# The first block's recurrent unit, cut into steps between the items of its attention, and a small product of the recurrence placed behind two transposes

## The chip, the cores and the metric

The kernel runs on one core of a Trainium2 chip. The metric is the device time of one execution in microseconds (us). A core has a matrix engine (PE in the views, TensorE), a vector engine (DVE), an activation engine (ACT), a general one (POOL), and a queue engine that only starts transfers (SP). Each works through its own list of instructions in order; semaphores make one wait for another. Matrix products go from the on-chip memory (here one big tile called arena) to eight banks of an accumulator memory (psum).

## The reference, cut to what matters

Two transformer-like blocks follow one another, all in 32-bit floats: 512 tokens, width 1024. The first block projects its input to six streams. Two of them go through a convolution and a gated linear recurrence (the recurrent unit), four through an attention with 8 heads; both results are normed, joined and projected.

```python
xa = causal_depthwise_conv(xa, conv_w, conv_b)
r = sigmoid(einsum(xa, w_a) + b_a);  i = sigmoid(einsum(xa, w_x) + b_x)
a = exp(-8 * r * softplus(-lam));    u = sqrt(1 - a * a) * (i * xa)
h[t] = a[t] * h[t-1] + u[t]
ya = rms_norm(h * silu(ga))
yb = rms_norm(dilated_attention(q, k, v) * silu(gb))
x = x + gate * rms_norm(concat(ya, yb) @ w_out)
```

The second block mixes a pooling branch, a differential attention and a two-way delta-rule recurrence, and ends in a mixture of 32 experts. In that recurrence every token also gets a bonus, whose coefficient is a product summed over each head's 64 channels: `coef = sum(r * k_mod * r_k)` per head.

## The kernel before, in words

The program is written out by hand for each engine; the order of the code is the order of the work. The stages of the first block are the modulation rows (`pre_`), the projections (`proj1_`), the recurrent unit (`lru_`), the attention (`att_`) and the output (`out1_`).

The recurrent unit works on four blocks m of 128 channels by 512 tokens. For each, DVE does the convolution (one `ts`, three `stt` of 512 elements per partition, signal `xc`), PE two gate products, ACT two sigmoids, then an exponential and a tanh (`th`), DVE an addition and a reciprocal (`rec`), two products (`ms`), ACT a square root, DVE a product, the scan and a product (`ya`). One block ends before the next begins, since all use the tiles tm[0] to tm[4]. After the fourth come the squares (`rsq`), a product with ones (`rs`), a root (`rsr`), a reciprocal and four scalings (`yan`). A short piece on 128x4 tiles ahead of it computes softplus(lam) on DVE.

The attention goes over 32 items x = (i, h): query tile i of 128 tokens and head h, with n = 128 (i + 1) keys. An item is a score product (`s1`), on DVE an addition of the mask and a maximum (`m1`), on ACT the exponential (`p1`), on PE i + 1 transposes (`pt1`), on ACT a copy, on PE i + 1 products with the values (`pv1`). The loop is skewed: in pass x PE does the scores of item x, the transposes of x - 2 and the values of x - 3. After each eighth item comes the output of query tile i: on DVE a reciprocal and two products (`yg`), on ACT a square and a root (`yr`), on DVE the norm (`yb`), then four transposes on PE.

Into both stages PE weaves the ada steps: 12 chunks of modulation weights, each 2 MB loaded by SP, in three steps q. Steps 0 and 1 are four products each with 32 output rows and 512 columns, step 2 adds a bias and gathers rows (two products with one or two output rows). 16 of the 36 steps stand in the recurrent unit, four behind each block's gates, and 20 in the attention, one per pass.

Psum banks are handed out in turn from a ring (`ps.take`): a new user waits until the one that had the bank is done with it. The recurrent unit has a ring of seven banks (LBANK), the attention one of five (ABANK), the ada steps one bank.

In the second block's recurrence two directions d, six chunks n each, are interleaved in a fixed order of steps; between the steps PE computes products of another stage (128x512, the gates of the merge). For a chunk, step g2 is 16 products into two banks, step kn transposes two key tiles into two banks, which ACT copies out. Each direction has a ring of only two banks. The coefficient product `co` has four matmuls with 8 columns; DVE adds or copies the result. It is there for 8 chunks (`lat`: four in each direction).

Of the kernel before, what the change touches and what calls it, by code (L numbers as in the profile page):

```python
# [11 lines left out]
ALU = mybir.AluOpType  # L12
ACT = mybir.ActivationFunctionType
# [319 lines left out]
def build(nc, T_):  # L333
# [18 lines left out]
    with ctx:  # L352
# [492 lines left out]
        def lru_gpsimd():  # L845
            G.wait_ge(T["f1", 3, 1])
            G.dma(wbd, T_["w_rg"], d_wbd.up("wbd"))
            G.dma(nbb, T_["norm_att"].partition_broadcast(128), d_na.up("na"))
            for j in range(4, 16):
                ada_gpsimd(j)  # L850

        def lru_tensor():
            steps = iter(ADA)
            for m in range(4):
                for j in range(2):
                    T.wait_ge(V["xc", m], d_wbd["wbd"], *ps.take(LBANK, "gate", m, j))
                    T.mm(ps["gate", m, j], wbd[:, c4(4 * j + m)], XC[:, m, :], True, True).then_inc("gate", m, j)
                for _ in range(4):
                    ada_tensor(*next(steps), MBANK)
            T.wait_ge(*ps.take(LBANK, "rs"))  # L860
            for m in range(4):
                T.wait_ge(A["rsq", m])
                T.mm(ps["rs"], ones, tm[m % 2], m == 0, m == 3).then_inc("rs", m)
            return steps

        def lru_scalar():
            steps = iter(ADA)
            A.wait_ge(V["lw1"])
            A.act(lw[2], lw[1], ACT.Exp).then_inc("lw2")
            for m in range(4):  # L870
                for j, (bn, tmp) in enumerate((("b_a", tm[0]), ("b_x", tm[1]))):
                    A.wait_ge(T["gate", m, j])
                    A.act(tmp, ps["gate", m, j], ACT.Sigmoid, bias=P[bn][:, m:m + 1])
                    ps.free(A.last(), "gate", m, j)
                A.wait_ge(V["lw"])
                A.act(tm[2], tm[0], ACT.Exp, scale=lw[7][:, m:m + 1])
                A.act(tm[3], tm[0], ACT.Tanh, scale=lw[6][:, m:m + 1]).then_inc("th", m)
                A.wait_ge(V["ms", m])
                A.act(tm[3], tm[3], ACT.Sqrt).then_inc("ms", m)
                for _ in range(4):  # L880
                    ada_scalar(*next(steps))
            A.wait_ge(V["ya", 3])
            for m in range(4):
                if m > 1:
                    A.wait_ge(T["rs", m - 2])
                A.act(tm[m % 2], XC[:, m, :], ACT.Square).then_inc("rsq", m)
            A.wait_ge(T["rs", 3])
            A.act(tm[2], ps["rs"], ACT.Sqrt, bias=eps[:, 0:1], scale=1.0 / 512).then_inc("rsr")
            ps.free(A.last(), "rs")
            return steps  # L890

        def lru_vector():
            lam, cw = P["lam"], P["conv_w"]
# [15 lines left out]
            for m in range(4):  # L909
                xc = XC[:, m, :]  # L910
                V.wait_ge(A["xa", m])
                V.ts(xc, XA[:, m, 1:513], cw[:, m:m + 1], P["conv_b"][:, m:m + 1], ALU.mult, ALU.add)
                for k in range(1, 4):
                    V.stt(xc, XA[:, m, 1 + k:513 + k], cw[:, 4 * k + m:4 * k + m + 1], xc, ALU.mult, ALU.add)
                V.then_inc("xc", m)
# [8 lines left out]
                V.tt(xc, tm[4], GA[:, m, :], ALU.mult).then_inc("ya", m)  # L924
            V.wait_ge(A["rsr"])
            V.rec(tm[2], tm[2])
            for m in range(4):
                V.stt(XC[:, m, :], XC[:, m, :], P["norm_rec"][:, m:m + 1], tm[2], ALU.mult, ALU.mult)
            V.then_inc("yan")
# [4 lines left out]
        def att_tensor(steps):  # L934
# [1843 lines left out]
```

## Time and profile before

| | |
|---|---|
| median of 3 runs | 2268.76 us (2268.49 to 2268.77) |
| the profiled execution, its own time | 2265.61 us |
| its span, first to last instruction | 2263.5 us |
| PE busy over the span | 1902.4 us (84%) |
| DVE, ACT busy | 814.9 us (36%), 519.8 us (23%) |
| mean granted TensorE clock | 0.893 |

The span is the time between the first and last instruction of the profiled execution; its own time contains 2.1 us more. The clock is the share of TensorE's full speed that was granted: 1.00 is 2.4 GHz and 0.50 is 1.2 GHz, and a value between them is a mixture over the window. PE's busy time is modelled at its ends, so that a busy PE need not be one at full rate.

### The profile page before, as it was taken

To read this page: it belongs to the slowest core of one execution; us is meant where nothing else is said; L and a number is where in the kernel's file an instruction comes from. 1 tells how busy PE (TensorE), PEld (TensorE's weight loads), DVE (VectorE), ACT (ScalarE), POOL (GpSimd) and SP (SyncE) were. 2 spreads that over 40 slices of the span, in tenths; PEclk is the share of its full clock that TensorE was granted. 3 is DMA by queue.
4 is the path that set the end of the run, shared out by engine and by line. 5 is a ranking of instruction groups with operands and counts; after the bars stand their busy time and mean duration, and the time that the engine had idled before them with its cause. 6 is when DMAs were issued, how large, how long until landed. Compare 5 with 4: busy or idle time off the path is not lost.

```text
span 2263.5 us, 29709 instructions
## 1 busy us (share of the span) xinstructions
PE 1902.4 (84%) x12822; PEld 1001.8 (44%) x12822; DVE 814.9 (36%) x1359; ACT 519.8 (23%) x957; POOL 82.5 (4%) x117
## 2 busy tenths in 40 slices
PE   5998569998998789978889889999974977777773
PEld 2443114643444555546666666664443332333231
DVE  2031533354645726434444544435335100000002
ACT  3001444321114512153233233113000000000001
POOL 0000000000000000020000000000000000000002
PEclk8999677599998899988899889999985999999997
DMA  8222343035111031031211111216415999999996
GB/s 338 75 74 75 112 159 139 27 137 218 59 37 38 0 135 47 0 127 43 67 49 54 62 43 49 90 35 270 159 64 224 416 428 426 426 427 426 428 427 242
DMA packets 49618, 376.37 MB, mean 166 GB/s; under 512 B 6033, under 2 KB 6177, under 8 KB 30795
## 3 DMA queue, kind: packets, MB, share of 16 engines
q1 hardware_dynamic: 36571, 317.85, 35.1%
q0 software_dynamic: 10032, 46.08, 5.6%
q10 hardware_dynamic: 2880, 10.49, 1.1%
q8 instruction: 103, 1.69, 0.3%
q14 instruction: 32, 0.26, 0.0%
HBM read 347.08 MB, written 31.51 MB: 167 GB/s over the span
## 4 chain that ended last, share of the span: by engine, by line
PE 40%; DMA 11%; DVE 8%; issue 2%; ACT 2%; POOL 0%; SPq 0%; DVEq 0%; ACTq 0%; POOLq 0%
PE psum L202 39%; DMA arena<-in_w 10%; DVE arena L149 4%; ACT arena L199 2%; DVE arena L159 1%; PE psum L205 1%; DVE arena L179 1%; DVE arena L167 1%; DVE arena L154 1%; DMA arena<-in_tok 0%; DVE arena L183 0%; DVE arena L187 0%; DVE arena L163 0%; DMA arena<-yd,arena 0%; DVE arena L175 0%
## 5 line engine op out<-in xcount | busy, mean ns | idle before, releaser
L202 PE MATMUL psum<-arena 64*64 64x32 f32 (+9 forms) x12174 | 1813.3, 372 | 303.0 <-ACT arena L199 104.2
L202 PEld LDWEIGHTS psum<-arena 64*64 64x64 f32 (+4 forms) x12174 | 922.5, 157 | 1135.3 <-issue 905.4
L199 ACT ACTIVATE arena<-psum 128x512 f32<-128x512 f32 (+6 forms) x389 | 206.5, 531 | 1195.9 <-PE psum L202 1083.2
L149 DVE TENSOR_TENSOR arena<-arena,psum 128x512 f32<-128x512 f32 (+1 forms) x136 | 75.5, 555 | 647.0 <-ACT arena L199 403.3
L199 ACT ACTIVATE arena<-arena 128x512 f32<-128x512 f32 (+10 forms) x242 | 135.4, 559 | 344.0 <-DVE arena L149 137.5
L149 DVE TENSOR_TENSOR arena<-arena 128x512 f32<-128x512 f32 (+11 forms) x312 | 195.4, 626 | 35.8 <-DMA arena<-in_norm_post 8.9
L149 DVE TENSOR_TENSOR arena<-psum,arena 128x256 f32<-128x256 f32 (+2 forms) x114 | 58.1, 509 | 253.8 <-PE psum L202 249.9
L159 DVE SCALAR_TENSOR_TENSOR arena<-arena 128x512 f32<-128x512 f32 (+5 forms) x138 | 111.4, 807 | 67.1 <-ACT arena L199 62.5
L205 PE MATMUL psum<-arena 128*128 128x128 f32 x648 | 108.3, 309 | 25.8 <-DVE arena L159 18.4
L205 PEld LDWEIGHTS psum<-arena 128*128 128x128 f32 x648 | 81.3, 157 | 93.3 <-issue 53.1
L199 ACT ACTIVATE arena<-psum,arena 128x128 f32<-128x128 f32 (+3 forms) x157 | 82.6, 526 | 173.0 <-PE psum L202 132.8
L167 DVE RECIPROCAL arena<-arena 128x1 f32<-128x1 f32 (+5 forms) x71 | 79.1, 1114 | 87.8 <-ACT arena L199 84.9
L154 DVE TENSOR_SCALAR arena<-arena 128x768 f32<-128x768 f32 (+9 forms) x156 | 50.0, 320 | 116.6 <-ACT arena L199 111.6
L199 ACT ACT_TABLE_LOAD x67 | 86.0, 1283 | 19.5 <-DMA arena<-gd 12.3
L163 DVE COPY arena<-psum 128x512 f32<-128x512 f32 (+2 forms) x76 | 47.6, 626 | 56.6 <-PE psum L202 31.1
L159 DVE SCALAR_TENSOR_TENSOR arena<-psum,arena 128x512 f32<-128x512 f32 (+3 forms) x44 | 23.7, 538 | 63.8 <-PE psum L202 62.6
L175 DVE TENSOR_REDUCE arena<-psum 128x1 f32<-128x768 f32 x32 | 30.7, 958 | 41.0 <-PE psum L202 38.5
L183 DVE STREAM_TRANSPOSE arena<-arena 128x512 f32<-128x512 f32 x60 | 42.7, 712 | 2.1
L179 DVE COPY_PREDICATED arena<-arena,psum 128x512 f32<-128x512 uint32 (+1 forms) x48 | 30.5, 636 | 25.4 <-PE psum L202 21.1
L142 POOL DMA_INDIRECT arena<-fd,arena x16 | 15.2, 948 | 512.7 <-PE psum L205 366.4
L139 POOL DMA_DIRECT2D arena<-kd x28 | 20.8, 750 | 341.5 <-DVE arena L149 328.4
L175 DVE TENSOR_REDUCE arena<-arena 128x1 f32<-128x32 f32 (+8 forms) x61 | 25.3, 414 | 6.1 <-PE psum L202 3.8
(46 smaller groups left out, 111.4 us busy)
## 6 DMA issues: line engine op xcount, KB each, us to landing
arena<-in_w SPq DMA_DIRECT2D x133, 2048.0 KB, 29.0
arena<-in_w SPq DMA_DIRECT2D x48, 256.0 KB, 3.0
yd<-arena ACTq DMA_DIRECT2D x16, 512.0 KB, 10.4
arena<-kd POOLq DMA_DIRECT2D x28, 256.0 KB, 3.9
gd<-arena SPq DMA_DIRECT2D x24, 256.0 KB, 3.1
arena<-gd SPq DMA_DIRECT2D x24, 256.0 KB, 8.4
yd<-in_zeros SPq DMA_DIRECT2D x1, 4096.0 KB, 18.6
arena<-in_w POOLq DMA_DIRECT2D x2, 2048.0 KB, 9.4
```

The lines of the kernel that those rows point to most:

```text
L139: self.e.dma_start(out, in_).then_inc(*signal)
L149: return self.ends(self.e.tensor_tensor(out, a, b, op))
L154: return self.ends(self.e.tensor_scalar(out, a, s1, None, op0))
L159: return self.ends(self.e.scalar_tensor_tensor(out=out, in0=a, scalar=s, in1=b, op0=op0, op1=op1))
L163: return self.ends(self.e.tensor_copy(out, a))
L167: return self.ends(self.e.reciprocal(out, a))
L175: return self.ends(self.e.tensor_reduce(out, a, AX, op, negate=negate))
L179: return self.ends(self.e.copy_predicated(out, mask, a))
L183: return self.ends(self.e.transpose(out, a))
L199: return self.ends(self.e.activation(out, a, func, **kw))
L202: return self.ends(self.e.matmul(out, lhs, rhs, start=start, stop=stop))
L205: return self.ends(self.e.transpose(out, a, ident))
```

## The change

The recurrent unit is no longer a stage of its own. Its functions now take a pass number x and do one piece of the work in that pass of the attention's loop. Block m has its gate products on PE and its sigmoids on ACT in pass 7m + 2, exponential and tanh in 7m + 3, addition and reciprocal on DVE in 7m + 4, the two products in 7m + 5, the root in 7m + 6, scan and products in 7m + 7. The convolutions are in passes 0 to 7, the final norm in passes 29 to 34. The softplus piece stays ahead of the loop on DVE. All 36 ada steps are in the attention, one per pass, and two in pass 1. PE computes the scores of item x + 1 in pass x; the score tile and the statistics have three buffers instead of two. The gate weights have memory of their own, so POOL starts their load and that of the attention's norm vector at once instead of behind the first transposes. Gates and `rs` take banks from ABANK. The transfers of out1 now wait for `yan` too. In the recurrence `co` stands behind the transposes of step kn, on PE and on DVE. The diff, cut:

```diff
 def lru_gpsimd():
-    G.wait_ge(T["f1", 3, 1])
     G.dma(wbd, T_["w_rg"], d_wbd.up("wbd"))
     G.dma(nbb, T_["norm_att"].partition_broadcast(128), d_na.up("na"))
...
-wbd = r0[:, 0:1024]
+wbd, Sb3, Pb3, sqj = ar.get(1024), ar.get(512), ar.get(512), ar.get(512)
-Sb, Pb, PTb, YB = sl[0:2], [sl[2], sl[3], tm[3]], sl[4:6], sl[6:8]
+Sb, Pb, PTb, YB = [*sl[0:2], Sb3], [sl[2], sl[3], Pb3], sl[4:6], sl[6:8]
...
-def lru_tensor():
-    steps = iter(ADA)
-    for m in range(4):
+def lru_tensor(x):
+    m = (x - 2) // 7
+    if x % 7 == 2 and m < 4:
         for j in range(2):
-            T.wait_ge(V["xc", m], d_wbd["wbd"], *ps.take(LBANK, "gate", m, j))
+            T.wait_ge(V["xc", m], d_wbd["wbd"], *ps.take(ABANK, "gate", m, j))
             T.mm(ps["gate", m, j], wbd[:, c4(4 * j + m)], XC[:, m, :], True, True).then_inc("gate", m, j)
-        for _ in range(4):
-            ada_tensor(*next(steps), MBANK)
-    T.wait_ge(*ps.take(LBANK, "rs"))
-    for m in range(4):
...
+    if x in (30, 31):
+        if x == 30:
+            T.wait_ge(*ps.take(ABANK, "rs"))
+        for m in (2 * x - 60, 2 * x - 59):
             T.wait_ge(A["rsq", m])
             T.mm(ps["rs"], ones, tm[m % 2], m == 0, m == 3).then_inc("rs", m)
...
+def lru_vector(x):
+    if x < 8:
...
+    m = (x - 4) // 7
+    if x % 7 == 4 and 0 <= m < 4:
         V.wait_ge(A["th", m])
         V.ts(tm[4], tm[3], 1.0, None, ALU.add)
         V.rec(tm[4], tm[4])
+    if x % 7 == 5 and 0 <= m < 4:
         V.stt(tm[3], tm[3], 2.0, tm[4], ALU.mult, ALU.mult).then_inc("ms", m)
-        V.tt(tm[1], tm[1], xc, ALU.mult)
+        V.tt(tm[1], tm[1], XC[:, m, :], ALU.mult)
+    m = x // 7 - 1
+    if x % 7 == 0 and 0 <= m < 4:
         V.wait_ge(A["ms", m])
         V.tt(tm[1], tm[1], tm[3], ALU.mult)
         V.scan(tm[4], tm[2], tm[1])
-        V.tt(xc, tm[4], GA[:, m, :], ALU.mult).then_inc("ya", m)
+        V.tt(XC[:, m, :], tm[4], GA[:, m, :], ALU.mult).then_inc("ya", m)
+    if x == 33:
         V.wait_ge(A["rsr"])
         V.rec(tm[2], tm[2])
+    if x == 34:
...
+scores(0)
 for x in range(len(IT1) + 3):
-    if x < len(IT1):
-        i, h = IT1[x]
+    if x + 1 < len(IT1):
+        scores(x + 1)
+    lru_tensor(x)
...
-    if (jq := next(steps, None)) is not None:
-        ada_tensor(*jq, MBANK)
+    for _ in range(1 + (x == 1)):
+        ada_tensor(*next(steps), MBANK)
...
-    n, o, s = 128 * (i + 1), LNC_OFF[i], Sb[x % 2]
+    n, o, s = 128 * (i + 1), LNC_OFF[i], Sb[x % 3]
     V.wait_ge(T["s1", x])
-    if x > 1:
-        V.wait_ge(A["p1", x - 2])
+    if x > 2:
+        V.wait_ge(A["p1", x - 3])
...
+lru_vector(x)
 if x % 8 == 4 and x > 8:
     gated((x - 12) // 8)
...
-    if step == "g2" and lat(d, n):
-        T.wait_ge(V["e2", d, n], *ps.take(ring, "co", d, n))
-        for m in range(4):
-            T.mm(ps["co", d, n][:, 0:8], B.e2[:, m, :], IRK[:, m, :], m == 0, m == 3)
-        T.then_inc("co", d, n)
 elif step == "kn":
     for j in range(2):
         T.wait_ge(*ps.take(ring, "kn", d, n, j))
         for m in range(4):
             T.tr(ps["kn", d, n, j][:, c4(m)], B.KB[:, j, m, :], ident)
         T.then_inc("kn", d, n, j)
+    if lat(d, n):
+        T.wait_ge(V["e2", d, n], *ps.take(ring, "co", d, n))
+        for m in range(4):
+            T.mm(ps["co", d, n][:, 0:8], B.e2[:, m, :], IRK[:, m, :], m == 0, m == 3)
+        T.then_inc("co", d, n)
...
-    elif lat(d, n):
+elif step == "kn":
+    if lat(d, n):
         V.wait_ge(T["co", d, n])
```

On DVE, at the beginning of the recurrent unit (the rows of 128x4 tiles end the softplus piece; 128x512 are tiles of the recurrent unit), there stood before:

```order
L159 SCALAR_TENSOR_TENSOR arena<-arena 128x4 x2
L154 TENSOR_SCALAR arena<-arena 128x4 x2
L155 TENSOR_SCALAR arena<-arena 128x512
L159 SCALAR_TENSOR_TENSOR arena<-arena 128x512 x3
L154 TENSOR_SCALAR arena<-arena 128x512
L167 RECIPROCAL arena<-arena 128x512
```

and now, where the rows that read psum are the scores of items 0 to 2, and the reductions their maxima:

```order
L159 SCALAR_TENSOR_TENSOR arena<-psum,arena 128x128
L175 TENSOR_REDUCE arena<-arena 128x1
L155 TENSOR_SCALAR arena<-arena 128x512
L159 SCALAR_TENSOR_TENSOR arena<-arena 128x512
L159 SCALAR_TENSOR_TENSOR arena<-psum,arena 128x128
L175 TENSOR_REDUCE arena<-arena 128x1
L159 SCALAR_TENSOR_TENSOR arena<-arena 128x512 x2
L159 SCALAR_TENSOR_TENSOR arena<-psum,arena 128x128
L175 TENSOR_REDUCE arena<-arena 128x1
```

The convolution is split in two pieces, and a score row and a maximum stand ahead of each.

On PE, in the recurrence, around the first coefficient product (64x128 are the products of step g2, 128x8 is `co`, 128x512 the woven products, L205 the transposes of the keys; the brackets name the semaphores waited for), there stood before:

```order
L202 MATMUL psum<-arena 64x128 [waits s_dve]
L202 MATMUL psum<-arena 64x128 x15
L202 MATMUL psum<-arena 128x8 [waits s_dve]
L202 MATMUL psum<-arena 128x8 x3
L202 MATMUL psum<-arena 128x512 [waits d_gw2,s_act]
L202 MATMUL psum<-arena 128x512
L202 MATMUL psum<-arena 64x32 x16
L202 MATMUL psum<-arena 64x64 x16
L202 MATMUL psum<-arena 128x512 x2
L205 MATMUL psum<-arena 128x128 [waits s_dve]
L205 MATMUL psum<-arena 128x128 x3
```

and now:

```order
L202 MATMUL psum<-arena 64x128 [waits s_dve]
L202 MATMUL psum<-arena 64x128 x15
L202 MATMUL psum<-arena 128x512 [waits d_gw2,s_act]
L202 MATMUL psum<-arena 128x512
L202 MATMUL psum<-arena 64x32 [waits s_dve]
L202 MATMUL psum<-arena 64x32 x15
L202 MATMUL psum<-arena 64x64 x16
L202 MATMUL psum<-arena 128x512 x2
L205 MATMUL psum<-arena 128x128 [waits s_dve]
L205 MATMUL psum<-arena 128x128 x3
L205 MATMUL psum<-arena 128x128 [waits s_dve]
L205 MATMUL psum<-arena 128x128 x3
L202 MATMUL psum<-arena 128x8 [waits s_act]
```

The product has moved behind the transposes, and what it waits for at its bank is ACT instead of DVE.

## Rows read from the trace of the kernel before

**Rows 1.** The page: span, busy tenths in 40 slices of 56.6 us.
```profile
span 2263.5 us, 29709 instructions
...
PE   5998569998998789978889889999974977777773
...
PEclk8999677599998899988899889999985999999997
DMA  8222343035111031031211111216415999999996
```

**Rows 2.** Windows of the two stages: busy us (instructions) by engine, clock, DMA share, GB/s.
```profile
217.50:318.30 100.80, 49.47 (x146) 10.24 (x144) 54.14 (x80) 41.74 (x51) 2.57 (x5) 0.71 0.39 143
318.30:356.00 37.70, 33.70 (x146) 11.63 (x146) 12.04 (x32) 18.70 (x50) 2.03 (x4) 0.86 0.55 195
356.00:370.00 14.00, 14.00 (x42) 4.58 (x41) 2.54 (x6) 4.30 (x13) 0.51 (x1) 0.51 0.23 97
370.00:387.00 17.00, 15.55 (x73) 6.46 (x72) 7.98 (x15) 9.67 (x20) 0.50 (x1) 0.99 0.33 124
387.00:447.30 60.30, 55.23 (x180) 38.48 (x180) 20.84 (x35) 23.76 (x49) 0.51 (x1) 0.50 0.00 1
```

**Rows 3.** Timeline of DVE, one block of channels: start us, busy us, idle before and releaser.
```profile
225.72 0.55 DVE L155 TENSOR_SCALAR arena<-arena 128x512 f32<-128x512 f32 x1
226.30 2.33 DVE L159 SCALAR_TENSOR_TENSOR arena<-arena 128x512 f32<-128x512 f32 x3
236.07 0.43 DVE L154 TENSOR_SCALAR arena<-arena 128x512 f32<-128x512 f32 x1 [7.45 <-ACT arena L199]
236.53 3.35 DVE L167 RECIPROCAL arena<-arena 128x512 f32<-128x512 f32 x1
...
254.82 0.43 DVE L154 TENSOR_SCALAR arena<-arena 128x512 f32<-128x512 f32 x1 [7.75 <-ACT arena L199]
```

**Rows 4.** Timeline of ACT in the same block.
```profile
233.26 1.28 ACT L199 ACT_TABLE_LOAD   x1
234.56 1.48 ACT L199 ACTIVATE arena<-arena 128x512 f32<-128x512 f32 x2
```

**Rows 5.** Timeline of PE in the attention, columns as in rows 3.
```profile
343.10 2.06 PE L202 MATMUL psum<-arena 128*32 128x512 f32 x12
...
363.17 4.13 PE L202 MATMUL psum<-arena 128*32 128x512 f32 x14
...
387.21 3.12 PE L202 MATMUL psum<-arena 128*128 128x64 f32 x8 [1.66 <-ACT arena L199]
...
429.36 3.81 PE L202 MATMUL psum<-arena 128*128 128x64 f32 x10
...
447.29 1.12 PE L205 MATMUL psum<-arena 128*128 128x128 f32 x4 [4.87 <-DVE arena L159]
```

**Rows 6.** Windows of the start, columns as in rows 2.
```profile
0.00:28.20 28.20, 8.23 (x44) 2.29 (x46) 0.81 (x6) 7.50 (x13) 1.48 (x6) 0.94 0.94 371
```

**Rows 7.** Timeline of PE at the start.
```profile
28.16 4.62 PE L202 MATMUL psum<-arena 128*32 128x512 f32 x24 [5.46 <-DMA arena<-in_w]
```

**Rows 8.** Timeline of POOL at the start.
```profile
36.63 0.53 POOL L139 DMA_DIRECT2D arena<-in_w_rg  x1 [34.05 <-PE psum L205]
```

**Rows 9.** Groups by form, 975 to 1525 us: busy, mean ns, idle before by releaser.
```profile
L202 PE MATMUL psum<-arena 128*128 128x8 f32 x64 | 12.3, 320 | 16.4 <-DVE arena L179 16.4
```

**Rows 10.** Timeline of PE around one coefficient product.
```profile
1260.44 7.77 PE L202 MATMUL psum<-arena 128*128 128x8 f32 x57 [3.06 <-DVE arena L179]
```

**Rows 11.** Timeline of DVE at the same place.
```profile
1259.65 1.59 DVE L179 COPY_PREDICATED arena<-arena,psum 128x512 f32<-128x512 uint32 x2
```

**Rows 12.** Timeline of ACT: two copies of transposed keys.
```profile
1050.00 1.29 ACT L199 ACTIVATE arena<-psum 128x512 f32<-128x512 f32 x2
```

**Rows 13.** Timeline of SP: the experts' weight loads.
```profile
1608.18 185.28 SPq L139 DMA_DIRECT2D arena<-in_w  x20
```

**Rows 14.** Window of the recurrence, columns as in rows 2.
```profile
975.00:1525.00 550.00, 500.14 (x8031) 345.76 (x8031) 247.93 (x421) 174.26 (x348) 28.11 (x41) 0.91 0.19 62
```

More of the change, by code:

```diff
@@ L874, in lru_scalar @@
                     ps.free(A.last(), "gate", m, j)
+            if x % 7 == 3 and m < 4:
                 A.wait_ge(V["lw"])
@@ L877, in lru_scalar, with lru_start_vector @@
                 A.act(tm[3], tm[0], ACT.Tanh, scale=lw[6][:, m:m + 1]).then_inc("th", m)
+            if x % 7 == 6 and m < 4:
                 A.wait_ge(V["ms", m])
                 A.act(tm[3], tm[3], ACT.Sqrt).then_inc("ms", m)
[L880 to L893, printed above, removed]
+            if x in (29, 30):
+                A.wait_ge(V["ya", 3])
+                for m in (2 * x - 58, 2 * x - 57):
+                    if m > 1:
+                        A.wait_ge(T["rs", m - 2])
+                    A.act(tm[m % 2], XC[:, m, :], ACT.Square).then_inc("rsq", m)
+            if x == 32:
+                A.wait_ge(T["rs", 3])
+                A.act(tm[2], ps["rs"], ACT.Sqrt, bias=eps[:, 0:1], scale=1.0 / 512).then_inc("rsr")
+                ps.free(A.last(), "rs")
+        def lru_start_vector():
+            lam = P["lam"]
             V.ts(lw[0], lam, -1.0, None, ALU.mult)
@@ L908, in lru_vector @@
             V.ts(lw[7], lw[5], -8.0, None, ALU.mult).then_inc("lw")
[L909 to L913, printed above, removed]
+        def lru_vector(x):
+            cw = P["conv_w"]
+            if x < 8:
+                m, xc = x // 2, XC[:, x // 2, :]
+                if x % 2 == 0:
+                    V.wait_ge(A["xa", m])
+                    V.ts(xc, XA[:, m, 1:513], cw[:, m:m + 1], P["conv_b"][:, m:m + 1], ALU.mult, ALU.add)
+                for k in ((1,), (2, 3))[x % 2]:
                     V.stt(xc, XA[:, m, 1 + k:513 + k], cw[:, 4 * k + m:4 * k + m + 1], xc, ALU.mult, ALU.add)
-                V.then_inc("xc", m)
+                if x % 2:
+                    V.then_inc("xc", m)
+            m = (x - 4) // 7
+            if x % 7 == 4 and 0 <= m < 4:
                 V.wait_ge(A["th", m])
@@ L967, in att_gated_tensor, with att_scalar @@
             T.then_inc("yt", i)
-        def att_scalar(steps):
+        def att_scalar():
+            steps = iter(ADA)
+            A.wait_ge(V["lw1"])
+            A.act(lw[2], lw[1], ACT.Exp).then_inc("lw2")
             for x in range(len(IT1) + 3):
@@ L986, in att_scalar @@
                     ps.free(A.last(), "pt1", x - 2)
-                if (jq := next(steps, None)) is not None:
-                    ada_scalar(*jq)
+                lru_scalar(x)
+                for _ in range(1 + (x == 1)):
+                    ada_scalar(*next(steps))
                 if 0 <= x - 3 < len(IT1) and IT1[x - 3][1] == 7:
@@ L991, in att_scalar @@
                     A.wait_ge(V["yg", i])
-                    A.act(tm[0], YB[i % 2], ACT.Square, accum_out=st1[:, 40 + i:41 + i])
+                    A.act(sqj, YB[i % 2], ACT.Square, accum_out=st1[:, 40 + i:41 + i])
                     A.act(st1[:, 44 + i:45 + i], st1[:, 40 + i:41 + i], ACT.Sqrt, bias=eps[:, 0:1],
@@ L2500, in vector_program @@
             proj1_vector()
-            lru_vector()
+            lru_start_vector()
             att_vector()
```

48 lines of the change are left out of this document (25 added, 23 removed).

## The prediction

> **What bounds the kernel now.** I read the page first, for which engine is busy where. The reader sees PE at 9 tenths over most slices, with dips in slices 5 to 7, and transfers at 9 tenths from slice 32 to the end [rows 1]. That end is the experts' weight stream. Could it swallow a gain made early? Its loads start at 1608.18, each behind a product that frees its buffer [rows 13], so the stream comes earlier by whatever the work ahead of it comes earlier. I count a gain ahead of it in full.
>
> Then I cut the place of the change into windows [rows 2]. The recurrent unit lasts from 217.5 to 318.3. PE is busy for 49.5 of its 100.8 us, DVE for 54.1, ACT for 41.7: no engine is full, it is a chain. The rows on DVE show it: 7.45 us of waiting for ACT ahead of the addition in the first block, 7.75 in the second, one block each 18.75 us (236.07 to 254.82) [rows 3]. The attention, 318.3 to 447.3, is the opposite: PE is busy for 33.7 + 14.0 + 15.6 + 55.2 = 118.5 of 129.0 us, and its gaps are small: 1.66 us on ACT behind an output chain, 4.87 us on DVE at the end [rows 5]. DVE adds 43.4 us there and ACT 56.4. Over both stages PE has 168.0 us of work in 229.8 us, DVE 97.5, ACT 98.2. So the recurrent unit's work fits into the attention's on DVE and ACT, and what can be won is PE's idle time, 61.8 us.
>
> In the recurrence PE is busy for 500 of 550 us [rows 14], and one group of eight coefficient products has 16.4 us of idle time ahead of it, all of it on DVE's predicated copy [rows 9].
>
> **The merged stage.** I build its end from PE's work.
> - Start: 217.5. The softplus piece still stands ahead of item 0 on DVE, until 225.7 [rows 3]: 8.2 us. PE has two score products and one ada step to do meanwhile, some 3 us.
> - PE's work: 168.0 us as measured at the old clocks, less those 3: 165.0. No product is added or taken away.
> - Gaps that stay: the last output chain ends in 4.87 us [rows 5].
> - Gaps that are new: in passes 4, 11, 18 and 25 DVE has the reciprocal and the addition of a block, 0.43 + 3.35 us [rows 3], ahead of the next item's maximum. In passes 11, 18 and 25 this is next to an output chain (passes 10, 18, 26), in pass 4 it has to wait for gates, sigmoids and exponential. Some of it is covered by the two items that PE has in hand (the products between two items' transposes take 2.06 us at n = 256, 4.13 at half the clock, 3.81 at n = 512 without an ada step [rows 5]). Between 0 and 3.8 + 1.7 us each, I take 2.5, for the cover was almost enough at the output chain whose gap is 1.66 us: 10.
> - Sum: 217.5 + 8.2 + 165.0 + 4.9 + 10 = 405.6.
>
> The clock changes this. In the last 60.3 us, without ada steps, PE was at 0.50 although it was busy; from 370 to 387, with ada steps on every item, at 0.99; from 356 to 370, with ada steps too but behind a gap, at 0.51 [rows 2]. The change puts an ada step on every one of those last items. If they all ran at the upper level, up to 27.6 of the 55.2 us would go; if none, 0. One of two stretches with ada steps had it, but the new gaps fall into it: I take a quarter, 7. The stage then ends at 398.6 instead of 447.3: 48.7 us won.
>
> **Tables.** ACT switches its function tables where exponentials meet sigmoids and roots. The order of the changed program has 28 table loads where before's has 25, up to the output stage. At 1.28 us each, with the next instruction starting 0.02 us behind [rows 4], that is 3.9 us more, on an engine with 98.2 us of work in about 181: hidden. If its cover were gone it would cost 3.9. The Trainium skill, on the page "ScalarE: Activation LUTs", section "What ACT_TABLE_LOAD costs", speaks against this change: it gives 1.28 us plus a drain, 2.66 us in all, for a switch, and its section "Rules for kernel authors" says to do all of one set before switching. By its figure the three loads would be 8 us, and all 28 some 75, an estimate that still fits beside PE; the trace shows the 1.28 and no drain behind it.
>
> **Start.** The transfers of 512 KB of gate weights and 256 KB of norm vector were started at 36.63 and after [rows 8]; now POOL starts them first thing, behind its two other loads. Until 28.2 the transfer engines are busy for 0.94 of the time at 371 GB/s [rows 6], and PE's third modulation row waits 5.46 us for its weights, until 28.16 [rows 7]. So 0.79 MB more ahead of that cost 0.79 MB / (371 / 0.94 GB/s) = 2.0 us (0 if they come in gaps). Where they were, they were hidden. I take 2.0 lost.
>
> **The coefficient product.** Before, PE waits at `co` for a bank that DVE frees with the first of its two predicated copies; the one at 1260.44 waited 3.06 us [rows 10], and DVE did that copy only at 1259.65, since it was still at the other work of g1 [rows 11]. Behind `co` other products were ready. Now they go first, and kn takes that bank some steps later. Won: up to 16.4 us [rows 9]. Lost: `co` waits for ACT's first copy of the keys, half of 1.29 us [rows 12], less the second four transposes that PE still does, so some 0.3 us in the direction where ACT is free and about 0.9 where it has just had other copies: 4 x 0.3 + 4 x 0.9 = 4.8. And in one direction the next step needs DVE as well, 0.5 us each: 2. Net 9.6 (bounds -5 and 16.4). DVE's own piece, on 8 columns, only moves.
>
> **Sum.** -48.7 + 2.0 - 9.6 = -56.3 us. Against the profiled execution's 2265.6 this is 2209.3. The median is 3.2 us above that execution, so I predict 2212 (2212.5, rounded down).
>
> **The rivals.**
> 1. The clock stays at the upper level in the last part, since the ada steps keep it there as from 370 to 387. A further 20.6 us go there, and 7 of the 14.0 between 356 and 370: 2212 - 27.6 = 2184. For it: 0.99 in that stretch. Against: each output chain leaves a gap, and the stretch behind one was at 0.51 for 14 us. 0.20.
> 2. The clock is lower than before: the gates and the ada steps no longer run in a block but thinly between short products, and the level is 1.2 GHz in most of the stage. Then the 7 us are not won, and the stretches that had 0.86 and 0.99 lose. The price of the half clock is 4.13 us for 14 products against 2.06 for 12 [rows 5], 0.295 to 0.172, a factor of 1.7. A mean clock c is 2c - 1 of the time at the upper level, so busy time there was 0.72 x 33.7 + 0.98 x 15.6 + 0.42 x 49.5 = 60.3 us; all of it at the lower is 42 us more: 2261. With half of it: 2240. 0.22.
> 3. The slower side: the chain of the recurrent unit is not hidden, but paid hop by hop. Every piece now stands in an in-order list ahead of the next item: a DVE that waits for `th` holds the next maximum, an ACT that waits for a gate holds the next exponential. There are 4 blocks of 5 hops and 4 in the final norm, 24. At 2.35 us each the whole gain is gone (56.3 / 24), and at 2.6 us the kernel is slower by 6: 2275. For it: the waits on ACT were 7.5 us per block. Against: a hop now has a whole item between its ends, at least 2 us of PE's work, and most have one in hand. 0.03.
> 4. The wait at `co` only moves to kn, which takes the same bank: the recurrence gives nothing, 2222. For it: the bank is the same. Against: PE has at least two steps and their woven products in between, and DVE's lateness was 3 us. 0.05.
>
> The forecast has 0.50.
>
> **Range.** The forecast's own parts go from 2196 (gaps 0, `co` 16) to 2230 (gaps 5.5 each, no clock gain). Reaching to the other cases, I give 2183 to 2243: it leaves out about half of rival 1, the farther part of rival 2 and rival 3. Less than 0.2% (4.5 us) is about what a measurement of this kernel can't tell from no change. Faster by more: 0.95; within: 0.02, from the far end of rival 2; slower: 0.03.
>
> **What would show it.** PE's last transposes of the attention, 447.29 before, should come near 401 (the start's loss included). In the stage PE should be busy over nine tenths, with gaps of some us behind passes 4, 11, 18 and 25, and DVE should have no wait of 7 us left. The clock of the last 50 us of the stage tells the forecast (0.6 to 0.7) from rival 1 (near 1) and rival 2 (0.5, and below 0.75 before). The third modulation row should start near 30.0. The group of `co` should have about 5 us ahead of it, on ACT, and the transposes of the keys little on DVE. The prediction fails if PE is idle between items because DVE or ACT is late, or if the stretch behind 975 comes no closer than the stage alone explains.

## The result and the profile after

The changed kernel takes 2208.41 us (median of four runs: 2200.1, 2202.5, 2214.3, 2215.3) against 2268.62 us for the kernel before on the same chip: ratio 0.9736, 95% interval 0.9693 to 0.9779. It is 60 us faster. The profile is of one of its longer executions, 2214.32 us with a span of 2212.4, so it shows 51.1 us of the gain.

The page, its lines in the order of [rows 1]. A slice is now 55.3 us:

```profile
span 2212.4 us, 29685 instructions
...
PE   5999799889998789979999999999875978777773
...
PEclk7999656799997899988999999999986999999997
...
DMA  8112433424111040031211111236226999999995
```

The dip of PE in slices 5 and 6 is filled (slices 5 to 7 had 5, 6 and 9 tenths in [rows 1] and have 7, 9 and 9 now), but the clock digits there are no higher: 6, 5 and 6, where before had 6, 7 and 7. Windows show what that means. They are cut at the same instructions in both traces: the start up to the first projection, the attention with the recurrent unit (the stage), and the recurrence. Before, whose windows in [rows 2] and [rows 14] were cut otherwise:

```profile
0.00:43.20 43.20, 20.10 (x129) 9.49 (x129) 10.38 (x26) 15.77 (x24) 2.55 (x8) 0.91 0.96 388
218.10:447.30 229.20, 167.34 (x581) 71.39 (x581) 97.53 (x166) 98.17 (x180) 6.13 (x12) 0.69 0.30 111
978.80:1525.80 547.00, 497.20 (x8027) 344.98 (x8028) 246.54 (x419) 170.62 (x342) 25.07 (x36) 0.91 0.19 63
```

And after:

```profile
0.00:47.35 47.35, 21.96 (x128) 12.34 (x128) 10.36 (x26) 15.73 (x24) 2.55 (x8) 0.80 0.96 386
222.20:423.80 201.60, 174.53 (x577) 67.71 (x577) 97.53 (x166) 101.44 (x183) 6.13 (x12) 0.66 0.34 126
954.85:1477.10 522.25, 483.07 (x8027) 335.30 (x8028) 246.70 (x419) 170.29 (x343) 25.31 (x37) 0.95 0.20 66
```

The start is 4.2 us longer, the stage 27.6 shorter, the recurrence 24.8 shorter. The stretch between the last two changes by 0.5, the one behind by 2.4, and 4.2 - 27.6 - 24.8 - 0.5 - 2.4 gives the 51.1. Length less PE's busy time is PE's idle time. In the stage it goes from 61.9 to 27.1 us, but the busy time grows by 7.2 at a lower clock. In the recurrence the idle time falls by 10.6, and the busy time by another 14.1 for the same products at a higher clock.

The timeline of PE after, the row of the start and the larger waits of the stage, to be read against [rows 5] and [rows 7]:

```profile
30.11 5.44 PE L202 MATMUL psum<-arena 128*32 128x512 f32 x24 [6.00 <-DMA arena<-in_w]
...
233.54 7.20 PE L202 MATMUL psum<-arena 18*1 18x512 f32 x10 [7.80 <-ACT arena L199]
...
248.38 5.00 PE L202 MATMUL psum<-arena 18*1 18x512 f32 x8 [3.81 <-ACT arena L199]
...
336.69 1.94 PE L202 MATMUL psum<-arena 128*32 128x512 f32 x8 [2.13 <-ACT arena L199]
...
423.79 1.12 PE L205 MATMUL psum<-arena 128*128 128x128 f32 x4 [5.62 <-DVE arena L159]
```

The last transposes start at 423.79 instead of 447.29. The wait of 7.80 us is in pass 1, the one with two ada steps: its second step gathers rows that ACT copies at 232.80, only behind two exponentials, and these wait for DVE, which takes the scores of item 0 at 229.48, when the softplus piece is done:

```profile
229.48 0.29 DVE L159 SCALAR_TENSOR_TENSOR arena<-psum,arena 128x128 f32<-128x128 f32 x1
...
232.80 0.60 ACT L199 ACTIVATE arena<-psum 128x512 f32<-128x512 f32 x1
```

The group of `co`, by form in the recurrence, against [rows 9]:

```profile
L202 PE MATMUL psum<-arena 128*128 128x8 f32 x64 | 8.5, 259 | 3.7 <-ACT arena L199 3.7
```

### The profile page after: what moved, and what is told of

Read it like the earlier page. It is cut to its first block, busy times and chain, and to the rows that moved or that the text cites. A ratio compares the mean times of both kernels' runs of the same rounds, so it can differ in the third digit from the quotient of the medians.

```text
span 2212.4 us, 29685 instructions
## 1 busy us (share of the span) xinstructions
PE 1895.1 (86%) x12822; PEld 990.4 (45%) x12822; DVE 815.0 (37%) x1359; ACT 522.5 (24%) x960; POOL 82.5 (4%) x117
## 4 chain that ended last, share of the span: by engine, by line
PE 41%; DMA 11%; DVE 8%; ACT 2%; issue 2%; POOL 0%; SPq 0%; DVEq 0%; ACTq 0%; POOLq 0%
PE psum L202 40%; DMA arena<-in_w 11%; DVE arena L149 3%; ACT arena L199 2%; DVE arena L159 1%; PE psum L205 1%; DVE arena L167 1%; DVE arena L154 1%; DVE arena L179 1%; DVE arena L163 0%; DVE arena L187 0%; DMA arena<-yd,arena 0%; DVE arena L183 0%; DVE arena L175 0%; DMA yd<-arena 0%
## 5 line engine op out<-in xcount | busy, mean ns | idle before, releaser
L202 PEld LDWEIGHTS psum<-arena 64*64 64x64 f32 (+4 forms) x12174 | 909.4, 155 | 1089.5 <-issue 906.7
L199 ACT ACTIVATE arena<-psum 128x512 f32<-128x512 f32 (+5 forms) x389 | 206.1, 530 | 1193.5 <-PE psum L202 1043.2
L149 DVE TENSOR_TENSOR arena<-arena,psum 128x512 f32<-128x512 f32 (+2 forms) x136 | 75.6, 556 | 645.6 <-ACT arena L199 405.9
L199 ACT ACTIVATE arena<-arena 128x128 f32<-128x128 f32 (+10 forms) x242 | 134.8, 557 | 305.6 <-DVE arena L149 138.7
L205 PE MATMUL psum<-arena 128*128 128x128 f32 x648 | 109.4, 311 | 27.4 <-DVE arena L159 19.6
L205 PEld LDWEIGHTS psum<-arena 128*128 128x128 f32 x648 | 82.7, 159 | 99.1 <-issue 54.7
L199 ACT ACT_TABLE_LOAD x70 | 89.8, 1283 | 19.3 <-DMA arena<-gd 12.1
L163 DVE COPY arena<-psum 128x512 f32<-128x512 f32 (+2 forms) x76 | 47.6, 626 | 70.8 <-PE psum L202 39.2
```

Source lines behind the costliest of these rows:

```text
L149: return self.ends(self.e.tensor_tensor(out, a, b, op))
L163: return self.ends(self.e.tensor_copy(out, a))
L199: return self.ends(self.e.activation(out, a, func, **kw))
L202: return self.ends(self.e.matmul(out, lhs, rhs, start=start, stop=stop))
L205: return self.ends(self.e.transpose(out, a, ident))
```

## The experiments

Twelve kernels ran beside the kernel before, whose median was 2264 to 2267 us there. Differences below are the ratio less 1, times 2265 us: by this the changed kernel is at -60.

### The two parts apart

The kernel before with `co` alone moved:

```diff
-                if step == "g2" and lat(d, n):
+            elif step == "kn":
...
+                if lat(d, n):
                     T.wait_ge(V["e2", d, n], *ps.take(ring, "co", d, n))
```

> The kernel before, with only the bonus coefficients co taken behind the transposes of the keys (the recurrent steps stay in one piece behind the attention). Theory A (the waits and the clock together): the 16.4 us that VectorE waited ahead of co go to about 4, TensorE waits some 10 us less in the recurrence of the next stage, its granted clock there rises from 0.91 to about 0.95 and its busy time falls by a further 14 us, as in the changed kernel; some 24 us faster, 2244 us. Rival B (only the waits count, and the higher clock of the changed kernel's recurrence comes from elsewhere, such as its earlier start or lower heat): 10 to 12 us faster, 2257 us, with the clock of that stretch still 0.91.

Measured: 2250.63 us, ratio 0.994 (0.9921 to 0.996), -14 us. That is near rival B's 10 to 12 and far from A's 24. The recurrence shows why: 533.3 us, between 547.0 and 522.3.

```profile
978.06:1511.39 533.33, 495.45 (x8027) 342.57 (x8028) 246.53 (x419) 170.66 (x342) 25.00 (x36) 0.92 0.20 65
```

Its idle time, 37.9 us, is even below the changed kernel's 39.2. The waits went as theory A said (3.2 us are left ahead of `co`, 11.9 us of idle time are gone), but PE's busy time is 12.4 us above the changed kernel's, and that lies for the most part in one place. PE's timeline there, first of this kernel:

```profile
1335.45 10.11 PE L202 MATMUL psum<-arena 64*64 64x128 f32 x116 [2.69 <-DVE arena L179]
1345.49 1.97 PE L205 MATMUL psum<-arena 128*128 128x128 f32 x8
```

and of the changed kernel at the same instructions:

```profile
1312.37 5.47 PE L202 MATMUL psum<-arena 64*64 64x128 f32 x116 [2.68 <-DVE arena L179]
1317.77 1.09 PE L205 MATMUL psum<-arena 128*128 128x128 f32 x8
```

The same 116 products behind the same wait, 2.69 and 2.68 us, take 10.11 us in one kernel and 5.47 in the other. The windows of 19 us from there, of this kernel and of the changed one:

```profile
1335.40:1354.40 19.00, 18.95 (x168) 13.65 (x168) 7.18 (x13) 2.56 (x5) 0.00 (x0) 0.50 0.09 29
```
```profile
1312.30:1331.30 19.00, 18.61 (x372) 14.31 (x372) 8.81 (x17) 4.43 (x7) 0.00 (x0) 1.00 0.14 43
```

All of one is at 1.2 GHz and all of the other at 2.4.

The other part alone is the changed kernel with `co` back at g2, the diff above turned round.

> The changed kernel with the coefficient product co back at step g2, as before; only the recurrent unit's move is left. The coefficients alone had won 13.4 us, the whole change 59.8. Theory A (the two parts are independent): 46 us faster than before, 2218 us, with the recurrence at 547 us and clock 0.91 as before. Rival B (the recurrence gains 11 us from the earlier merge by way of the clock, since the kernel with co alone had one stretch of 18 us at 0.50 that the changed kernel does not have): the recurrence is near 536 us here too, and the kernel 57 us faster, 2207 us.

Measured: 2228.84 us, ratio 0.9838 (0.9817 to 0.9859), -37 us. The two windows, the stage and the recurrence:

```profile
219.75:412.50 192.75, 164.20 (x577) 63.46 (x576) 97.53 (x166) 101.43 (x183) 6.11 (x12) 0.71 0.36 131
942.48:1489.23 546.75, 496.82 (x8027) 344.53 (x8028) 246.56 (x419) 170.24 (x343) 25.30 (x37) 0.91 0.19 63
```

The recurrence is as before, so the earlier merge by itself gives it nothing: theory A held there, rival B fell, though A's 46 us were too many. The parts add up to -50, the whole is -60 (its interval allows -50). The profiles show a difference of that size: the recurrence with `co` moved takes 533.3 us with the stretch at 0.50 and 522.3 without. Of the ten profiled kernels that have both parts, it was there in two (below), and in eight not. Note also the stage: 192.75 us here, 201.6 in the changed kernel's profile, with the same instructions; PE is busy for 164.2 us of it here and for 174.5 there, and idle for 28.6 and 27.1.

### The start

The changed kernel with one line back ahead of the loads of the small tables:

```diff
+            G.wait_ge(T["f1", 3, 1])
             G.dma(wbd, T_["w_rg"], d_wbd.up("wbd"))
```

> The changed kernel, with GpSimd again waiting for the third product of the rotary table's first layer (f1 of 3) ahead of the loads of the recurrent unit's small tables, as in the kernel before. Theory A (the start lost 2 us to the transfers and 2 us more to the lower clock behind the longer wait): the third modulation row stands near 28.2 us again instead of 30.1, the first projection starts near 43.2 instead of 47.4, and the kernel is about 4 us faster than the changed one, 2204 us. Rival B (only the transfers): 2 us faster, 2206. Rival C (the small tables now come too late for the recurrent unit's first steps inside the attention): the early passes wait, and nothing is won.

Measured: 2202.74 us, ratio 0.9737 (0.9704 to 0.977), the same as the changed kernel's. Its windows of the start and of the stage:

```profile
0.00:43.12 43.12, 18.27 (x128) 9.32 (x128) 10.36 (x26) 15.77 (x24) 2.54 (x8) 0.90 0.96 389
218.30:411.20 192.90, 164.30 (x578) 63.50 (x576) 97.46 (x166) 101.70 (x183) 6.10 (x12) 0.71 0.36 131
```

The mechanism showed as written: the third modulation row starts at 28.28 us, the projections at 43.12. But the kernel's time doesn't show the 4 us. A kernel whose executions lie up to 15 us apart hides them, and the other kernels without the wait that have the merged stage started their projections at 44.7 to 47.7, so part of the 4.2 varies by itself. What is safe is the row at 29.9 to 30.3 in every profiled one of them, against 28.1 to 28.4 where the wait stands: the 2 us of the transfers. Rival C's late tables don't show: the first two long waits of the stage are 7.78 and 3.83 us, as in the changed kernel.

### More work on TensorE

One useless product ahead of each score product; the scores overwrite it:

```diff
                 T.wait_ge(*ps.take(ABANK, "s1", x))
+                T.mm(ps["s1", x], ident, QT[:, 0, :], True, True)
```

> The changed kernel with one more full product (128x512, identity times a slice of the queries, written to the scores' bank and overwritten by the scores themselves) ahead of each of the 32 score products of the first block's attention: 14 us of TensorE work at full clock, 27 at half. Theory A (the merged stage is held back by TensorE's clock, which is 0.66 there because its work is thinly spread): the granted clock of the stretch from 222 to 424 us rises to 0.75 or more, and the stage becomes no longer, or up to 10 us shorter. Rival B (it is bound by TensorE's work, at a clock that does not answer to it): the stage is 14 to 27 us longer, 2222 to 2241 us. Rival C (it is bound by VectorE's and ScalarE's chain): the idle time of TensorE, 27 us, takes the work up and the time stays within 5 us at an unchanged clock.

Measured: 2196.76 us, ratio 0.9695 (0.9671 to 0.9718), -69 us: by the ratios 9 us faster than the changed kernel, with more work. The two intervals overlap, so the safe part is that it is not slower. And the work was larger than I had written. At full clock in the projections 27 records of such products took 10.46 us, and a product is two records, so 32 are 25 us, or 50 at half the clock. The stage:

```profile
220.40:412.90 192.50, 168.21 (x645) 62.68 (x643) 97.48 (x166) 101.83 (x183) 6.11 (x12) 0.87 0.36 132
```

The clock rises to 0.87, and at least 25 us more work leaves the busy time where it was. The stage is 9 us shorter than in the changed kernel's profile and as long as in the executions at 192.8. Theory A held, B fell. C too: the clock did not stay, and the idle time is still 24.3 us.

The same in the kernel before, for its last 16 items only (`if x > 15:` ahead of the product):

> The kernel before with one more full product (128x512, overwritten by the scores) ahead of each of the last 16 score products of its attention, where no modulation steps are left from item 20 on and the granted clock was 0.50 for 60 us. It adds 16 products of 0.85 us at full clock, 14 us, or 27 us at half. Theory A (the clock answers to how much TensorE is given in the stretch): the clock of that stretch rises above 0.8, its own 55 us of work shrink by 15 to 25 us, and the kernel is 0 to 12 us faster than before, 2252 to 2264. Rival B (the clock does not answer to it): 14 to 27 us slower, 2278 to 2291.

Measured: 2266.51 us, ratio 0.9997 (0.9984 to 1.001): 12.5 us of work at full clock cost no time. Rival B fell. Of theory A the direction held, but the clock from 387 to the end of the stage is 0.78, not above 0.8, and the time is at the lower end of its 0 to 12 us. The window of 29.4 us behind the output chain at 387, of the kernel before and of this one:

```profile
387.00:416.40 29.40, 29.19 (x88) 19.00 (x88) 10.61 (x19) 12.67 (x28) 0.51 (x1) 0.50 0.00 1
```
```profile
387.00:416.40 29.40, 27.38 (x124) 14.42 (x122) 15.38 (x26) 15.61 (x34) 0.51 (x1) 1.00 0.00 1
```

The wait of 1.66 us at 387.21 [rows 5] is gone, and the clock stays up. It falls at the next such wait and has 0.56 from there to the end of the stage:

```profile
416.45 5.51 PE L202 MATMUL psum<-arena 128*128 128x64 f32 x12 [2.08 <-ACT arena L199]
```

In the kernel before it fell at 387 and stayed low to the end of the stage, for 60 us, although PE was busy for 55.2 of them. The Trainium skill, page "TensorE: Matmul & The Clock Gate", section "A second HAM failure mode: psum-queue depth-cycling", says that frequent short idle times between groups of products are enough to make the clock swing. The traces agree in kind: a short wait, 1.66 and 2.08 us, stands right at each of these two falls. They don't show that such a wait alone decides it, for the same wait of 2.7 us had the clock at 0.50 behind it in one kernel and at 1.00 in another (above).

### Grouping the modulation steps

The number of ada steps per pass follows a pattern instead of being one each, on PE and ACT alike. Three patterns keep the sum over three passes; the fourth only moves the doubled step from pass 1 to pass 0.

```diff
+        ada_share = lambda x: 1 + x if x < 2 else (0, 1, 2)[x % 3]   # first pattern
+        ada_share = lambda x: (2, 1, 0)[x % 3]                       # second
+        ada_share = lambda x: (2, 0, 1)[x % 3] + (x == 34)           # third
+        ada_share = lambda x: 1 + (x == 0)                           # fourth
...
-                for _ in range(1 + (x == 1)):
+                for _ in range(ada_share(x)):
```

> The changed kernel, with the modulation steps that lie between the passes of the first block's attention grouped: two in one pass, one in the next, none in the third, instead of one in each. Their sum is the same. Theory A (clock): TensorE's work comes in denser pieces, more stretches stand at full clock, and the stage is 3 to 10 us shorter, about 2208 us or less. Rival B (the clock doesn't answer to grouping at this scale): within 3 us. Rival C (two modulation steps behind each other put ScalarE's copies ahead of the exponentials and make waits of their own like the 7.8 us in the second pass): slower by 2 to 10 us.

> The changed kernel with the modulation steps grouped as two, one, none in passes 0, 1, 2 and so on through the whole attention (the kernel with two, none, one was 18 us faster than the changed one). The same number of steps in every three passes. Theory A (it is the grouping that raises TensorE's clock): again 14 to 22 us faster than the changed kernel, 2183 to 2191 us, and the wait of 7.8 us in the second pass is shorter, since the third step no longer stands behind the second in one pass. Rival B (the gain depends on where each group falls against the recurrent unit's pieces and the output chains): less than 10 us, 2195 us or more. Rival C (the third step, close behind the pair, waits for ScalarE's copies): waits of 2 us at each group, 20 us slower than A.

> The changed kernel with the modulation steps grouped as two, none, one from pass 0 on, the same grouping as in the kernel that was 18 us faster than the changed one, but one pass earlier by phase. Theory A (grouping): 14 to 22 us faster than the changed kernel, 2183 to 2191 us, stage clock near 0.79. Rival B (phase against the recurrent unit's pieces decides): less than 10 us faster, 2195 us or more, with the clock below 0.72.

> The changed kernel with only the doubled modulation step moved from the second pass to the first; the rest stay one per pass. The third step of the first chunk then no longer stands right behind the second on TensorE, where the changed kernel had a wait of 7.8 us for ScalarE's copy. Theory A (the 28 us of the pattern two, none, one are this gap and the grouping together, and the grouping is the larger part): 4 to 10 us faster than the changed kernel, 2197 to 2203 us. Rival B (the whole gain of that pattern is the first gap and the clock behind it): 20 us or more, below 2188. Rival C (TensorE then waits for VectorE's convolution instead, 8.2 us, as it did with that pattern): within 3 us of the changed kernel.

Measured, in this order: 2186.92 us (ratio 0.9655, 0.9637 to 0.9674, -78 us), 2188.71 (0.9665, 0.9642 to 0.9688, -76), 2175.67 (0.9599, 0.9581 to 0.9616, -91), 2210.04 (0.9742, 0.9716 to 0.9768, -58). So the three groupings gain 18, 16 and 31 us over the changed kernel, and moving the doubled step gains nothing. The stages of the three groupings, one line from each trace:

```profile
220.20:395.90 175.70, 140.32 (x577) 57.62 (x577) 97.48 (x166) 101.66 (x183) 6.11 (x12) 0.79 0.39 144
```
```profile
222.60:395.00 172.40, 144.29 (x578) 59.68 (x576) 97.54 (x166) 101.50 (x183) 6.13 (x12) 0.78 0.40 147
```
```profile
220.30:385.30 165.00, 135.25 (x579) 58.05 (x577) 97.54 (x166) 101.47 (x183) 6.13 (x12) 0.83 0.42 154
```

and of the fourth:

```profile
222.60:424.36 201.76, 170.28 (x578) 65.12 (x577) 97.50 (x166) 101.45 (x183) 6.13 (x12) 0.69 0.34 126
```

With grouping, idle time is 35.4, 28.1 and 29.8 us, no less than the 27.1 of the changed kernel: what shrank is the busy time, by 30 to 39 us, at 0.78 to 0.83 (by 20 to 29 us against the executions whose stage took 192.8). Theory A of the first three held in kind, but the first and the third gained more than their expectations' 3 to 10 and 14 to 22 us; the third is the first's order shifted by a pass, so phase matters beside grouping. For the fourth rival C's time came true, but not its way: the first gap only shrank from 7.80 to 5.84 us, and another of 3.84 us that the changed kernel didn't have stood in a later pass.

The third pattern with the product of the filler experiment added:

> The best pattern so far (modulation steps two, none, one: 2176 us, clock of the stage 0.83, TensorE idle 30 of 165 us) with one more full product ahead of each of the 32 score products: 27 us of TensorE work more at full clock. Theory A (the clock still has something to give): clock 0.9 or more, and the stage within 8 us of before the filler, 2168 to 2184. Rival B (at 0.83 the clock has little left, so that useless work now costs itself where TensorE is not idle): 8 to 20 us slower, 2184 to 2196.

Measured: 2180.9 us, ratio 0.9618 (0.9602 to 0.9634), -87 us: 4 us slower than the pattern alone (the intervals overlap), inside A's range and near B's.

```profile
222.40:388.85 166.45, 152.25 (x644) 60.51 (x643) 97.50 (x166) 101.44 (x183) 6.13 (x12) 0.93 0.41 152
```

At 0.93, with 25 us more work, the stage is only 1.5 us longer, and idle time takes up most of it (29.8 to 14.2). So at 165 us PE's work no longer sets the stage's length. What is left are its waits on DVE and ACT; that their chain is the limit is argued from this and not shown, and none of its hops was singled out.

### The piece ahead of the stage

The third pattern, with the softplus piece ahead of the last gated product of the projections, on DVE and its exponential on ACT; the second kernel has the start's wait back as well.

```diff
+                if (c, m) == PROJ1[-1]:
+                    lru_start_vector()
...
-            lru_start_vector()
             att_vector()
```

> The pattern two, none, one, and the softplus piece of the recurrent unit (29 short operations of VectorE, 6 us, and one exponential of ScalarE) moved ahead of the last gated product of the projections, where VectorE waits 6.18 us for ScalarE's sigmoid. Theory A (the stage starts by that piece later than it could, the lead-in of my forecast): the wait of 8.2 us of TensorE for VectorE near 232 us falls to about 2, and the kernel is 6 us faster than with the pattern alone, 2170. Rival B (the earlier passes are bound by TensorE's clock or ScalarE instead): less than 2 us. Rival C (the exponential's two table loads, 2.6 us, make the last sigmoid late): slower by up to 3 us.

> As the kernel before it in this call (pattern two, none, one, softplus ahead of the last gated product), with GpSimd's wait ahead of the loads of the small tables back as in the kernel before the change. In the first comparison this took the start of the projections from 47.35 back to 43.12 us. Theory A: the projections start at 43.1 instead of 45 to 47.5, 2 to 4 us faster, 2166 to 2168. Rival B (the small tables come too late for the first passes): no gain.

Measured: 2182.74 us (ratio 0.9634, 0.9611 to 0.9658, five runs from 2176 to 2192) and 2180.63 (0.9625, 0.961 to 0.964): no faster than the pattern alone, 2175.67, and by the ratios 6 to 8 us slower. Stage and recurrence of the first:

```profile
222.20:386.44 164.24, 139.37 (x577) 58.93 (x577) 93.01 (x139) 101.25 (x182) 6.13 (x12) 0.81 0.42 154
917.09:1450.42 533.33, 495.60 (x8027) 342.56 (x8028) 246.58 (x419) 170.09 (x342) 25.06 (x36) 0.92 0.20 65
```

The wait that theory A named did fall, from 8.20 to 1.97 us, and the idle time by 4.9, but the busy time rose by 4.1: the clock took it, and the stage is only 0.8 us shorter, as rival B had it. And the recurrence, where not an instruction differs, has the 533.3 us again, with the same stretch at 0.50, and so has the other kernel (533.2). That costs 11 us in the profiled executions, more than the wait was worth. For the kernel's time all three theories fall; they looked only at the stage. Of the first kernel's five executions the fastest, 2176.1, is as fast as the pattern alone, so the stretch may be missing in some of them; only one was profiled. In the second kernel the modulation row and the projections came back to 28.39 and 43.77 us, from 30.08 and 47.36, but its time can't be told from the first one's: theory A's 2 to 4 us are not shown.

## Why the prediction was right, and in which parts it was off

The forecast was 2212 us and the time 2208.41. That the sum came out so near is luck: two errors against each other were nearly equal, the stage 21 us too much and the recurrence 15 too little.

- **Start, 2.0 us lost.** The row is at 30.11, 0.1 from the text, and at 28.28 with the wait put back. The first projection came 4.2 us later, since the clock of that window was 0.80 instead of 0.91; this I had not counted.
- **Merged stage, 48.7 us won: mis-sized.** The mechanism was right in kind: most of PE's waits go, DVE and ACT keep their 97.5 and 101.4 us. The size was 27.6 us in the profiled execution and 36 in the two other traces with the same stage. The forecast's stage holds 161 us of PE's work (168.0 less 7) and 20 of idle time (8.2 less the 3 of work, 4.9, 10). Measured are 174.5 and 27.1 us in the profiled execution, 164.2 and 28.6 in the two others.
- **The idle time of the stage, 27.1 instead of 20.** Ahead of the products at 233.54 PE is idle for 8.9 us. Some 4.8 of them pass until the softplus piece is done, where I had 5.2. The other 4.1 are the path behind it (two maxima, a piece of the convolution, an exponential, a copy), which the sum doesn't have. The waits from pass 4 to 28 add up to 12.6 us instead of 10, but mostly not by the reciprocal that I made responsible. In pass 4, ACT works without a pause from 240.89 until the copy for which PE waits 3.81 us, and DVE's reciprocal starts only behind that copy's start:

```profile
240.89 0.28 ACT L199 ACTIVATE arena<-psum 128x128 f32<-128x128 f32 x1 [2.48 <-PE psum L205]
241.19 1.28 ACT L199 ACT_TABLE_LOAD   x1
...
243.97 1.28 ACT L199 ACT_TABLE_LOAD   x1
...
247.73 0.60 ACT L199 ACTIVATE arena<-psum 128x512 f32<-128x512 f32 x1
```
```profile
248.13 3.35 DVE L167 RECIPROCAL arena<-arena 128x512 f32<-128x512 f32 x1
```

  The waits in passes 10, 11 and 25 (1.45, 0.83, 1.61) stand behind such full stretches of ACT too. The reciprocal stands ahead of 1.5 us in pass 13 alone, an output chain ahead of 2.7 us in pass 20, and behind pass 18 there is no wait.
- **The clock.** For the last part I gave 0.6 to 0.7, and there it is right, 0.67 in the last 50 us. The quarter that I took was 7 us because I halved the 55.2; by my own factor of 1.7 all of it would have been 23 us and a quarter 6. What failed in the profiled execution is the step before it, that PE's 165 us of work would take what they took "at the old clocks". The stage in two windows, its first 141 us and its last 60:

```profile
222.20:363.50 141.30, 120.48 (x385) 43.24 (x386) 71.85 (x133) 75.35 (x139) 4.10 (x8) 0.67 0.40 146
363.50:423.80 60.30, 54.04 (x193) 24.48 (x191) 25.68 (x34) 26.09 (x44) 2.03 (x4) 0.64 0.21 78
```

  Before, the windows ahead of the last 60 us had 0.71, 0.86, 0.51 and 0.99 [rows 2]; now all that work runs at 0.67. Rival 2, thin mixing, was right in kind but not in size: 21 to 42 us of busy time were its price, 7.2 above the old value the measured one, and in the two other traces PE's busy time was 3 us below the old value. Rival 1 did not occur: an ada step on every item did not keep the clock up. It fell right behind the wait of 1.61 us in pass 25 and stayed at 0.50 for 41 us:

```profile
362.60:403.60 41.00, 40.36 (x113) 17.27 (x112) 17.71 (x24) 17.64 (x31) 1.01 (x2) 0.50 0.19 72
```

- **Tables.** The page has 70 loads instead of 67, 1283 ns each as before, and in the stage ACT is busy for 101.4 of 201.6 us. But "hidden" holds only for the average: two loads, 2.6 us, are in the stretch of ACT that ends the wait of 3.81 us in pass 4, two in the one ahead of the 1.61 in pass 25, and one in the one ahead of the 1.45 in pass 10. How much the kernel would gain without them is open, for no kernel without them was run.
- **The coefficient product, 9.6 us won.** As waiting time this is right: PE's idle time in the recurrence fell by 10.6, and `co` waits 3.7 us for ACT, where I had 4.8. But the recurrence gave 24.8, since the clock there was 0.95 instead of 0.91. This term was too small by 15 us. It is 13.7 us when the stretch of 19 us falls to half clock (`co` alone: 11.9 of idle and 1.8 of busy time) and 24.8 when it doesn't, so the removed waits alone don't explain the clock. Rival 4 is out, rival 3 too.
- **What would show it.** The last transposes came at 423.8 instead of 401. PE is busy for 87% of the stage, below the nine tenths I wrote. DVE still has a long wait, 13.85 us ahead of the reciprocal of the final norm:

```profile
413.40 3.35 DVE L167 RECIPROCAL arena<-arena 128x512 f32<-128x512 f32 x1 [13.85 <-ACT arena L199]
```

  This is not free. The reciprocal and the four scalings behind it end at 419.9, and only then does DVE begin the last output chain, while PE's last product ended at 418.2:

```profile
413.14 5.03 PE L202 MATMUL psum<-arena 128*32 128x512 f32 x28
```
```profile
419.94 0.20 DVE L167 RECIPROCAL arena<-arena 128x8 f32<-128x8 f32 x1
```

  That is some 2 of the 5.62 us at the stage's end. The sign of failure that I had written down, PE idle between items because DVE or ACT is late, is there too, with the 12.6 us above, but they are few beside the 61.9 us of idle time before. So the total is no proof of the steps: of its three terms only the start's, the 2.0 us of the transfers, was well sized.

## What to carry over

Count a removed wait twice, once as idle time and once for what the clock does to the work behind it, which was as large again here (10.6 and 14.1 us in the recurrence), was next to nothing with `co` alone (11.9 and 1.8) and can also go the other way. When short pieces are woven together, try them in small groups before spreading them evenly: the same steps in pairs were worth 16 to 31 us more here than one per pass. Before more waits are removed, useless work added to a stage tells what bounds it: if the stage doesn't get longer, it is the clock or another engine's chain, not the amount of TensorE's work.

## What the runs showed of the hardware that was not expected

- Products that do nothing can cost nothing: with 25 us of them in its stage the changed kernel was not slower (ratio 0.9695 against 0.9736, overlapping intervals), and 12.5 us in the kernel before left it at 0.9997. Where the stage's clock was at 0.83 already, 25 us of them cost 4 us, again with overlapping intervals.
- The same instructions behind the same wait (2.69 and 2.68 us) ran at 0.50 for 19 us in three kernels and at 1.00 in others. Within the kernel with `co` alone it seems to be there each time (2249.7 to 2253.0 us in four runs), but the kernel with the softplus moved spreads over 15.6 us in five. It doesn't follow the time at which the stretch begins (1272.3, 1274.5 and 1335.4 us with it, 1273.4 and 1312.4 without), and in the two cases with the softplus moved the only further edit lies 700 us ahead of the recurrence. What decides it stays open.
- A busy engine can stay at 1.2 GHz: in the kernel before for 60 us at 92% busy [rows 2], until the stage's end, and in the changed kernel for 41 us at 98%.
